# An encoder step: first C/D weights loaded in the stage before, three score blocks counted by GpSimd, ties of all blocks marked by GpSimd

## The chip, the cores and the metric

The kernel runs on one core of a Trainium2 chip, as one program. Times are device microseconds of a whole execution; less is better. Engines: PE is TensorE (matmuls), DVE is VectorE, ACT is ScalarE, POOL is GpSimd, and SP issues most of the DMAs. "Lines" are lines of the kernel before.

## What is computed

Two layers of a streaming encoder over 2048 prompt frames and 64 sample frames of width 1024. The second layer (C/D) projects its input to queries, keys, values, gates and to a small indexer. For every query frame the indexer scores all admissible keys, and the D attention of that frame sees only the 256 keys with the highest scores:

```python
def dsa_attend(q, qi, wi, qpos, k, v, ki, kpos, topk, t5_d):
    dots = jnp.einsum('bqhe,bke->bqhk', qi, ki)
    score = jnp.einsum('bqh,bqhk->bqk', wi, jax.nn.relu(dots))
    score = jnp.where(admissible, score, NEG_INF)
    _, sel = lax.top_k(score, topk)
    ...
```

Where scores are equal to the 256th, `top_k` takes the ones with the smaller index. The kernel needs no index list, only a mask of the selected keys.

## The kernel before

The stages follow each other, each ended by a meeting of all engines: the A/B layer, its attention and its mix; then `mix_out` of the first layer, `index_stage`, `project_cd`, the attentions C and D, and the last mix. The change touches `index_stage` (lines 2346 to 2570), `top_k` (2573 to 2750) and `project_cd` (2753 to 2915).

**Blocks.** The frames are 17 blocks of 128 rows. Blocks 2 to 16 need a selection. `SEL_BLOCKS` lists them as 3 to 11, then 2, then 12 to 16, and n counts along this list; block b has a score tile of 128 partitions and (b + 1) x 128 columns (`widths[n]`), 384 to 2176, 19,200 columns in all.

**index_stage** computes the indexer's projections (`plan.proj`: T units with the 512 columns of `W_t` as weights, N units with `W_n`) and the scores, in an order written out by a planner. The T units of the first 128 weight columns come last (`plan.tail`). SP loads the weights and then stores each unit's result in order.

**project_cd** does two things at once. TensorE (`multiply`, lines 548 and 551) computes 74 units of the C/D projection: 40 T units (four groups of 5 pieces, twice) and 34 N units, 16 matmul records each, in float32, into 8 PSUM banks. ScalarE copies each unit out (`evacuate`, line 2838) and SP stores it (2807). Meanwhile `top_k` finds the 256th largest score of every row.

**The search** (`search`, `signs`) is a bisection over the 32 bits of the float, all blocks at once, with one threshold a row and block in `thr`. In every step VectorE counts the scores that reach the threshold, block by block (line 2621; the first NOWN = 9 of the list, blocks 3 to 11), while ScalarE does it with the sum of signs for the last N_SIGN = 6 (line 2659; blocks 2 and 12 to 16). After the third count VectorE prepares the next trial in `tx` with an XOR (2625) and keeps the last count (`remember`, 2647). At the end it waits for all counts, decides (`pred`, 2629) and sets the thresholds (2638), for which both engines wait.

**The masks** (`masks`, `take_sides`, `leave`, `send`). A tail on VectorE (2667 to 2700) corrects the sign blocks: a count, a mark and a minimum for each of the six. Then a loop over the 15 blocks. VectorE marks the scores equal to the threshold (`ties`, 2707, into one of two `junk` buffers), numbers them by a running sum (2714), works out the room (2719), and selects (2723) with the signs that ScalarE took (2738). ScalarE scales the mask and writes it out (`leave`, 2744), SP sends it. The marks of block n + 1 are made behind the running sum of block n.

**ScalarE's order** is fixed. The evacuations are dealt out to the steps of the search by LEAD and PACE, and those left over to the mask loop, behind the leave of a block. In the search a step's first evacuation stands in front of its fourth sign and the others in front of its last:

```python
        STEPS, LEAD, PACE, EARLY, TILES = 32, 4, 0.56, 4, 6
        while int(LEAD + u * PACE) < STEPS:
            in_step[int(LEAD + u * PACE)].append(u)
            u += 1
```

Before, units 0 to 49 leave during the search, 50 to 53 right after it, 54 to 73 in the mask loop. GpSimd only sets 15 small constants in this stage (2728).

## Time and profile before

| | us |
|---|---|
| median of 3 runs | 3863.88 (3859.64 to 3863.9) |
| profiled execution | 3855.95, span of its instructions 3854.2 |
| TensorE busy | 3611.3 (94%) |
| VectorE busy | 2036.2 (53%) |
| ScalarE busy | 1622.6 (42%) |
| GpSimd busy | 691.1 (18%) |
| project_cd, from its first small constant to the last leave's end | 2306.8 to 2811.0 |

Busy shares are means over the whole kernel. Each stage has limits of its own, and a stage ends when the last of its engines does. TensorE's matmuls are pipelined, so that busy time there includes overlap. The granted clock is TensorE's, as a share of 2.4 GHz.

### The profile page before, as it was taken

To read this page: it belongs to the slowest core of one execution; us is meant where nothing else is said; L and a number is where in the kernel's file an instruction comes from. 1 tells how busy PE (TensorE), PEld (TensorE's weight loads), DVE (VectorE), ACT (ScalarE), POOL (GpSimd) and SP (SyncE) were. 2 spreads that over 40 slices of the span, in tenths; PEclk is the share of its full clock that TensorE was granted. 3 is DMA by queue.
4 is the path that set the end of the run, shared out by engine and by line. 5 is a ranking of instruction groups with operands and counts; after the bars stand their busy time and mean duration, and the time that the engine had idled before them with its cause. 6 is when DMAs were issued, how large, how long until landed. Compare 5 with 4: busy or idle time off the path is not lost. (4 is left out here: it accounts for less than half of the span.)

```text
span 3854.2 us, 50563 instructions
## 1 busy us (share of the span) xinstructions
PE 3611.3 (94%) x17937; PEld 2607.2 (68%) x17937; DVE 2036.2 (53%) x5023; ACT 1622.6 (42%) x2526; POOL 691.1 (18%) x475
## 2 busy tenths in 40 slices
PE   7999999989999999997998979899969899999798
PEld 6899999977776666664886745444446555556576
DVE  3311111128885444443321479999968777777432
ACT  5101100115454344333331469998457444444432
POOL 4110000012222111110431100000022432212342
PEclk9999999989999999998999999999979899999899
DMA  5522222144443222213442111101242411100443
GB/s 159 173 78 69 68 70 68 59 89 103 98 107 93 55 72 70 58 35 111 158 147 80 59 44 51 54 34 65 86 120 80 102 36 40 26 12 20 147 167 120
DMA packets 198855, 316.61 MB, mean 82 GB/s; under 512 B 24776, under 2 KB 140768, under 8 KB 193528
## 3 DMA queue, kind: packets, MB, share of 16 engines
q1 hardware_dynamic: 178928, 252.51, 22.0%
q0 software_dynamic: 12352, 34.36, 3.5%
q10 hardware_dynamic: 7344, 26.74, 1.9%
q8 instruction: 134, 2.20, 0.2%
q14 instruction: 97, 0.79, 0.1%
HBM read 212.89 MB, written 112.23 MB: 84 GB/s over the span
## 5 line engine op out<-in xcount | busy, mean ns | idle before, releaser
L1064 PE MATMUL attAB_p_o<-attAB_pt,attAB_v 128*65 128x512 f32 (+4 forms) x1120 | 432.1, 483 | 3.3 <-ACT attAB_pt L1113 3.3
L1156 DVE TENSOR_REDUCE attAB_mx<-attAB_p_s 128x1 f32<-128x512 f32 (+2 forms) x360 | 209.5, 609 | 298.1 <-PE attAB_p_s L997 187.4
L2621 DVE TENSOR_SCALAR_CACHE_REDUCE cd_junk<-score,cd_thr 128x512 bf16<-128x512 f32 (+8 forms) x288 | 350.4, 1275 | 1.3 <-DVE cd_thr L2638 0.2
L450 DVE COPY ab_stage<-ab_pA 128x256 f32<-128x256 f32 (+2 forms) x118 | 58.6, 496 | 543.2 <-PE ab_pA L208 542.7
L2659 ACT ACTIVATE cd_side<-score,cd_thr 128x384 bf16<-128x384 f32 (+2 forms) x192 | 322.3, 1679 | 24.0 <-DVE cd_thr L2638 16.5
L1040 PE MATMUL attAB_p_t<-attAB_q_a,attAB_k_a 128*128 128x512 f32 (+4 forms) x560 | 301.1, 542 | 12.8 <-DVE attAB_s_t L1203 11.5
L207 PE MATMUL ab_pA<-ab_W_lo,h_hi 128*128 128x256 f32 x1088 | 307.9, 283 | 0.0
L208 PE MATMUL ab_pA<-ab_W_hi,h_lo 128*128 128x256 f32 x1088 | 307.9, 283 | 0.0
L206 PE MATMUL ab_pA<-ab_W_hi,h_hi 128*128 128x256 f32 x1088 | 307.9, 283 | 0.0
L295 ACT ACTIVATE ab_stage<-ab_pA 128x256 f32<-128x256 f32 (+2 forms) x98 | 41.7, 426 | 591.7 <-PE ab_pA L208 578.6
L1713 PE MATMUL attD_p_o<-attD_pt,attD_v 128*65 128x512 f32 (+1 forms) x548 | 281.3, 594 | 1.8 <-ACT attD_pt L1802 1.8
L548 PE MATMUL cd_pA<-hT_cd,cd_W 128*128 128x448 f32 (+1 forms) x640 | 234.8, 530 | 28.3 <-ACT cd_stage L2838 15.2
L1802 ACT ACTIVATE attD_pt<-attD_s_t 128x512 f32<-128x512 f32 (+1 forms) x306 | 178.3, 602 | 154.4 <-DVE attD_s_t L1919 151.4
L551 PE MATMUL cd_pA<-cd_W,hT_cd 128*128 128x512 f32 x544 | 236.2, 596 | 6.2 <-ACT cd_stage L2838 5.6
L1113 ACT ACTIVATE attAB_pt<-attAB_p_t 128x512 f32<-128x512 f32 (+3 forms) x328 | 171.1, 543 | 163.9 <-PE attAB_p_t L1041 114.4
L206 PE MATMUL ab_pA<-h_hi,ab_W_hi 128*128 128x448 f32 (+1 forms) x640 | 229.9, 359 | 7.9 <-DVE ab_W_lo L220 7.9
L2187 PE MATMUL mix_pY<-mix_W_hi,mix_m_hi 128*128 128x512 f32 x544 | 219.5, 404 | 12.1 <-DVE mix_m_lo L2234 12.1
L207 PE MATMUL ab_pA<-h_lo,ab_W_hi 128*128 128x448 f32 (+1 forms) x640 | 228.4, 357 | 0.0
L208 PE MATMUL ab_pA<-h_hi,ab_W_lo 128*128 128x448 f32 (+1 forms) x640 | 228.3, 357 | 0.0
L548 PEld LDWEIGHTS cd_pA<-hT_cd,cd_W 128*128 128x128 f32 x640 | 124.1, 195 | 138.4 <-issue 98.5
L2188 PE MATMUL mix_pY<-mix_W_lo,mix_m_hi 128*128 128x512 f32 x544 | 216.2, 397 | 0.0
L2189 PE MATMUL mix_pY<-mix_W_hi,mix_m_lo 128*128 128x512 f32 x544 | 216.1, 397 | 0.0
(354 smaller groups left out, 8452.0 us busy)
## 6 DMA issues: line engine op xcount, KB each, us to landing
mix_o<-t_o SPq DMA_DIRECT2D x34, 512.0 KB, 4.4
mix_gate<-t_gate SPq DMA_DIRECT2D x68, 256.0 KB, 4.8
ab_W_raw<-in_w_ab SPq DMA_DIRECT2D x16, 1024.0 KB, 5.7
attAB_raw<-t_k SPq DMA_DIRECT2D x30, 544.0 KB, 6.1
attAB_raw<-t_q SPq DMA_DIRECT2D x30, 544.0 KB, 7.9
ab_front<-in_x ACTq DMA_DIRECT2D x17, 512.0 KB, 3.7
t_gate<-ab_stage SPq DMA_DIRECT2D x68, 128.0 KB, 1.7
t_v<-ab_stage SPq DMA_DIRECT2D x68, 128.0 KB, 1.7
```

What stands on the lines that cost most here:

```text
L206: nc.tensor.matmul(out, lh, rh, start=(k == 0), stop=False)
L207: nc.tensor.matmul(out, lh, rl, start=False, stop=False)
L208: last = nc.tensor.matmul(out, ll, rh, start=False, stop=(k == KT - 1))
L548: last = nc.tensor.matmul(pA[s][:, 0:end - begin], W[j % 2][:, k, c * P:(c + 1) * P], hT[:, k, begin:end], start=(k == 0), stop=(k == KT - 1))
L551: last = nc.tensor.matmul(pA[s][:, 0:w], hT[:, k, r * P:(r + 1) * P], W[j % 2][:, k, 0:w], start=(k == 0), stop=(k == KT - 1))
L1040: nc.tensor.matmul(out, hi[:, ks], q_a[j][:, cols], start=(x == 0), stop=False)
L1064: done = nc.tensor.matmul(p_o[u % 2][0:VW, i0 * w:(i0 + n) * w], left, pt[c % NPT][:, at * w:(at + n) * w], start=(c == plan.chunks_of[u][ ...
L1713: nc.tensor.matmul(p_o[u % 2][0:VW, 0:w], left, pt[c % NPT][:, 0:w], start=(c == first), stop=(c == last)).then_inc(valued, 1)
L2187: nc.tensor.matmul(out, m_hi[s][:, k, :], W_hi[:, k, cols], start=(k == 0), stop=False)
L2188: nc.tensor.matmul(out, m_hi[s][:, k, :], W_lo[:, k, cols], start=False, stop=False)
L2621: nc.vector.tensor_scalar(junk[nth % 2][:, 0:widths[n]], sc[n][:], T[:, n:n + 1], None, ALU.is_ge, ALU.add, accum_out=cnt[s % 2][:, n:n + ...
L2659: nc.scalar.activation(side[0][:, 0:widths[n]], sc[n][:], ACT.Sign, bias=T[:, n:n + 1], accum_out=cnt[s % 2][:, n:n + 1]).then_inc(signed, 1)
```

## The change

- `W_t`, the weight tile of the index stage, is now allocated outside and also serves as the first weight buffer of `project_cd`. SP loads the first C/D weights into it during the index stage: three quarters once the last unit that needs the old ones is staged, the last quarter after the last unit. `project_cd` then only signals that they are there.
- N_SIGN is 5, so block 2 is counted by VectorE. The list of blocks stays the same.
- GpSimd counts the first three blocks (3, 4, 5: 512, 640 and 768 columns). It writes 0/1 marks in bfloat16 into the buffer `rank`, padded to 768 columns with zeros, and adds the halves onto each other three times (384, 192, 96 columns for each of the three). VectorE sums the 3 x 96 that are left into the counts. VectorE itself counts blocks 6 to 11 and 2.
- The XOR for `tx` becomes a two-input instruction, an XOR with an OR against a zero tile, and stands after VectorE's third own count.
- In the mask loop GpSimd makes the marks of the ties for all 15 blocks.
- LEAD is 1: units 0 to 55 leave during the search, 56 to 59 right after it, 60 to 73 in the mask loop. A step's first evacuation stands in front of its third sign.

```diff
-N_SIGN = 6
+N_SIGN = 5
-SEL_BLOCKS = [*range(FIRST_SEL + 1, NB - N_SIGN + 1), FIRST_SEL, *range(NB - N_SIGN + 1, NB)]
+SEL_BLOCKS = [*range(FIRST_SEL + 1, NB - N_SIGN), FIRST_SEL, *range(NB - N_SIGN, NB)]
+N_POOL = 3
...
+                after = d.w_cd[0].rearrange("(k p) c -> p k c", p=P)
                 for p, (kind, c, x) in enumerate(plan.proj):
                     sp.wait_ge(staged, p + 1)
+                    if p == plan.tail - 1:
+                        for t in (1, 2, 3):
+                            sp.dma_start(W_t[:, :, t * P:(t + 1) * P], after[:, :, t * P:(t + 1) * P]
+                                         ).then_inc(next_in, 16)
+                    if p == NP - 1:
+                        sp.dma_start(W_t[:, :, 0:P], after[:, :, 0:P]).then_inc(next_in, 16)
...
+    NDVE = NOWN - N_POOL
+    WIDE = (SEL_BLOCKS[N_POOL - 1] + 1) * P
+    HALVINGS = 3
+    LEFT = WIDE >> HALVINGS
+    marks = rank[:].bitcast(BF16)[:, 0:N_POOL * WIDE].rearrange("p (n w) -> p n w", n=N_POOL)
...
-            for n in range(NOWN):
+            for n in range(N_POOL, NOWN):
...
-                if n == 2 and s >= 1:
+                if n == N_POOL + 2 and s >= 1:
                     undo = 3 * 2 ** (bit - 1) if bit >= 1 else 1
-                    nc.vector.tensor_scalar(tx[:], thr[:], undo, None, ALU.bitwise_xor).then_inc(tried, 1)
+                    nc.vector.scalar_tensor_tensor(tx[:], thr[:], undo, none[:], ALU.bitwise_xor, ALU.bitwise_or
+                                                   ).then_inc(tried, 1)
                     remember(dve, s - 1)
-            dve.wait_ge(counted, (s + 1) * NOWN)
+            dve.wait_ge(marked, (s + 1) * (N_POOL + HALVINGS))
+            nc.vector.tensor_reduce(cnt[s % 2][:, 0:N_POOL], marks[:, :, 0:LEFT], AX.X, ALU.add).then_inc(pooled, 1)
+            dve.wait_ge(counted, (s + 1) * NDVE)
+            dve.wait_ge(pooled, s + 1)
             dve.wait_ge(signed, (s + 1) * N_SIGN)
...
+    def count_by_pool(pool):
+        for n in range(N_POOL - 1):
+            nc.gpsimd.memset(marks[:, n, widths[n]:WIDE], 0.0).then_inc(blanked, 1)
+        pool.wait_ge(ready, SETUP)
+        for s in range(STEPS):
+            done = s * (N_POOL + HALVINGS)
+            if s >= 1:
+                pool.wait_ge(turned, s)
+            for n in range(N_POOL):
+                nc.gpsimd.tensor_scalar(marks[:, n, 0:widths[n]], sc[n][:], T[:, n:n + 1], None, ALU.is_ge
+                                        ).then_inc(marked, 1)
+            if s == 0:
+                pool.wait_ge(blanked, N_POOL - 1)
+            for k in range(HALVINGS):
+                half = WIDE >> (k + 1)
+                pool.wait_ge(marked, done + N_POOL + k)
+                nc.gpsimd.tensor_tensor(marks[:, :, 0:half], marks[:, :, 0:half], marks[:, :, half:2 * half], ALU.add
+                                        ).then_inc(marked, 1)
...
-        def ties(n):
-
-            if n >= 2:
-                dve.wait_ge(outed, n - 1)
-            nc.vector.tensor_scalar(junk[n % 2][:, 0:widths[n]], sc[n][:], T[:, n:n + 1], UNIT, ALU.is_equal, ALU.mult
-                                    ).then_inc(equal, 1)
-        ties(0)
...
-            if n + 1 < NSEL:
-                ties(n + 1)
...
+    def ties_by_pool(pool):
+        pool.wait_ge(fixed, 2 + 2 * N_SIGN + 6)
+        pool.wait_ge(counted, STEPS * NDVE + N_SIGN)
+        for n in range(NSEL):
+            if n >= 2:
+                pool.wait_ge(outed, n - 1)
+            nc.gpsimd.tensor_scalar(junk[n % 2][:, 0:widths[n]], sc[n][:], T[:, n:n + 1], UNIT, ALU.is_equal, ALU.mult
+                                    ).then_inc(equal, 1)
...
-        W = [sb(f"W{j}", [P, KT, BANK]) for j in range(2)]
+        W = [W_t, sb("W1", [P, KT, BANK])]
...
-        STEPS, LEAD, PACE, EARLY, TILES = 32, 4, 0.56, 4, 6
+        STEPS, LEAD, PACE, EARLY, TILES = 32, 1, 0.56, 4, 6
...
-                load(0)
+                sp.wait_ge(w_free[0], 1)
+                sp.sem_inc(w_in[0], 16)
                 load(1)
...
-                    at = {3: in_step[s][0:1], N_SIGN - 1: in_step[s][1:]}
+                    at = {2: in_step[s][0:1], N_SIGN - 1: in_step[s][1:]}
...
                 set_widths(pool)
+                count_by_pool(pool)
+                ties_by_pool(pool)
```

## Rows read from the trace of the kernel before

**Rows 1.** Timeline of ScalarE, end of the stage (start us, us, engine, line)

```profile
2808.96 2.01 ACT L2744 ACTIVATE score<-cd_junk 128x2176 bf16<-128x2176 bf16 x1
```

**Rows 2.** The page's groups (count, busy us, mean ns, idle before and releaser)

```profile
L1156 DVE TENSOR_REDUCE attAB_mx<-attAB_p_s 128x1 f32<-128x512 f32 (+2 forms) x360 | 209.5, 609 | 298.1 <-PE attAB_p_s L997 187.4
...
L548 PE MATMUL cd_pA<-hT_cd,cd_W 128*128 128x448 f32 (+1 forms) x640 | 234.8, 530 | 28.3 <-ACT cd_stage L2838 15.2
...
L551 PE MATMUL cd_pA<-cd_W,hT_cd 128*128 128x512 f32 x544 | 236.2, 596 | 6.2 <-ACT cd_stage L2838 5.6
```

**Rows 3.** Timeline of TensorE in the stage, two of its nine pieces

```profile
2315.78 97.38 PE L548 MATMUL cd_pA<-hT_cd,cd_W 128*128 128x320 f32 x272 [12.79 <-DMA cd_W<-in_w_cd]
...
2724.07 84.36 PE L551 MATMUL cd_pA<-cd_W,hT_cd 128*128 128x512 f32 x192 [2.73 <-ACT cd_stage L2838]
```

**Rows 4.** Timeline of VectorE, the tail and the end of the mask loop

```profile
2685.67 0.61 DVE L2672 TENSOR_SCALAR_CACHE_REDUCE cd_junk<-score,cd_thr 128x384 bf16<-128x384 f32 x1
...
2716.37 0.49 DVE L2707 TENSOR_SCALAR cd_junk<-score,cd_thr 128x512 bf16<-128x512 f32 x1
...
2805.00 2.48 DVE L2723 SCALAR_TENSOR_TENSOR cd_junk<-cd_rank,cd_room,cd_side 128x2176 bf16<-128x2176 f32 x1 [0.47 <-DVE cd_room L2719]
```

**Rows 5.** Instructions of line 2638 (min/median/max ns, first and last start)

```profile
L2638 DVE SCALAR_TENSOR_TENSOR cd_thr<-cd_pred,cd_tx x31: 174/174/175, 2330.5 to 2685.1; 128x15 int32<-128x15 int32 x31
```

**Rows 6.** Timeline of VectorE, second step of the search

```profile
2321.61 0.17 DVE L2625 TENSOR_SCALAR cd_tx<-cd_thr 128x15 int32<-128x15 int32 x1
...
2321.76 1.14 DVE L2621 TENSOR_SCALAR_CACHE_REDUCE cd_junk<-score,cd_thr 128x896 bf16<-128x896 f32 x1
...
2330.48 0.17 DVE L2638 SCALAR_TENSOR_TENSOR cd_thr<-cd_pred,cd_tx 128x15 int32<-128x15 int32 x1
```

**Rows 7.** Timeline of ScalarE, the same step

```profile
2319.20 0.61 ACT L2659 ACTIVATE cd_side<-score,cd_thr 128x384 bf16<-128x384 f32 x1 [0.73 <-DVE cd_thr L2634]
...
2319.94 1.68 ACT L2659 ACTIVATE cd_side<-score,cd_thr 128x1664 bf16<-128x1664 f32 x1
...
2329.82 0.18 ACT L2659 ACTIVATION_READ_ACCUMULATOR cd_side<-score,cd_thr 128x1 f32 x1
```

**Rows 8.** Timeline of SP's queue, last stores of the index stage

```profile
2217.29 58.13 SPq L2408 DMA_DIRECT2D t_kq<-ix_stage  x5
```

**Rows 9.** Window of 2 us behind TensorE's gap at 2724 (busy, granted clock)

```profile
2725.00:2727.00 2.00, 2.00 (x4) 0.61 0.29 111
```

**Rows 10.** Groups of GpSimd by form over the whole kernel

```profile
L2145 POOL TENSOR_TENSOR mix_gate<-mix_gate,mix_sig 128x1024 f32<-128x1024 f32 x32 | 76.4, 2389 | 170.7 <-ACT mix_sig L2096 170.7
...
L1573 POOL TENSOR_TENSOR attD_near_t<-attD_bias_t,attD_msk_t 128x1024 f32<-128x1024 f32 x33 | 69.9, 2137 | 182.6 <-ACT attD_msk_t L1778 182.2 <-DVE attD_bias_t L1858 0.4
...
L379 POOL CAST ab_front<-ab_front 8x2176 fp32r<-8x2176 f32 x2 | 4.0, 1993 | 46.9 <-DMA t_logf<-ab_front 43.5 <-DMA t_nf<-ab_front 3.4
```

**Rows 11.** Timeline of VectorE at three places outside the stage

```profile
14.92 1.36 DVE L479 TENSOR_TENSOR ab_wf_lo<-ab_stage,ab_wf_hi 128x64 fp32r<-128x64 f32 x1
...
3017.82 0.69 DVE L1881 CUSTOM_DVE_ANT_0 attD_junk<-attD_p_s,attD_msk 128x512 bf16<-128x512 f32 x1 [0.15 <-PE attD_p_s L1664]
...
3083.85 2.40 DVE L1846 TENSOR_TENSOR attD_c_b<-attD_raw,attD_c_a 64x2048 fp32r<-64x2048 f32 x1
```

**Rows 12.** Timeline of GpSimd at the same places, and one dependent pair

```profile
13.86 2.34 POOL L340 TENSOR_TENSOR h_lo<-ab_front,h_hi 128x1024 fp32r<-128x1024 f32 x1 [0.48 <-ACT h_hi L290]
...
2851.21 2.37 POOL L1554 TENSOR_TENSOR attC_q_a<-attC_q_raw,attC_q_a 64x1024 fp32r<-64x1024 f32 x1 [0.17 <-POOL attC_q_a L1554]
...
3017.65 4.07 POOL L1562 TENSOR_TENSOR attD_near<-attD_bias,attD_msk 128x2048 f32<-128x2048 f32 x1 [3.19 <-DMA attD_bias<-t_bias_d]
...
3084.18 6.02 POOL L1562 TENSOR_TENSOR attD_near<-attD_bias,attD_msk 128x2048 f32<-128x2048 f32 x1
```

**Rows 13.** Groups of VectorE in the mask loop, 2716 to 2815 us

```profile
L2707 DVE TENSOR_SCALAR cd_junk<-score,cd_thr 128x512 bf16<-128x512 f32 (+14 forms) x15 | 13.0, 866 | 4.7 <-ACT score L2744 4.7
...
L2719 DVE TENSOR_SCALAR cd_room<-cd_sums,cd_left 128x1 f32<-128x1 f32 x15 | 3.1, 208 | 3.4 <-ACT cd_side L2738 3.4
```

More of the change, by code:

```diff
@@ L2343, in score, with index_stage @@
         return u + 1
-def index_stage(nc, d, hT, sc):
+def index_stage(nc, d, hT, sc, W_t):
     plan = IndexPlan()
@@ L2354, in index_stage @@
         sb, ps, sem = allocate(nc, st, "ix")
-        W_t, W_n = sb("W_t", [P, KT, BANK]), sb("W_n", [P, KT, VW_W])
+        W_n = sb("W_n", [P, KT, VW_W])
         stage = [sb(f"stage{s}", [P, BANK]) for s in range(2)]
@@ L2367, in index_stage @@
         wn_in, products, staged, adm_in = sem("wn_in"), sem("products"), sem("staged"), sem("adm_in")
+        next_in = sem("next_in")
         stored = [sem(f"stored{k}") for k in range(2)]
@@ L2411, in _ @@
                 wait_stored(sp, NP)
+                sp.wait_ge(next_in, CT * 16)
             @block.gpsimd
@@ L2585, in top_k @@
     zero = sb("zero", [P, 1])
+    none = sb("none", [P, NSEL], I32)
     junk = [sb(f"junk{k}", [P, ROWS], BF16) for k in range(2)]
@@ L2596, in top_k @@
         "fixed", "equal", "ranked", "roomed", "sided", "chosen", "outed", "sent", "widths_set"))
+    marked, blanked, pooled = sem("marked"), sem("blanked"), sem("pooled")
     UNIT = 2.0 ** -12
@@ L2599, in top_k @@
     NOWN = NSEL - N_SIGN
-    SETUP = 5 + N_SIGN
+    NDVE = NOWN - N_POOL
[3 more added lines that the diff above has]
+    marks = rank[:].bitcast(BF16)[:, 0:N_POOL * WIDE].rearrange("p (n w) -> p n w", n=N_POOL)
+    SETUP = 6 + N_SIGN
     T = thr[:].bitcast(F32)
@@ L2606, in search @@
         nc.vector.memset(zero[:], 0.0).then_inc(ready, 1)
+        nc.vector.memset(none[:], 0).then_inc(ready, 1)
         nc.vector.memset(first[:, 0:NOWN], 2 ** 30).then_inc(ready, 1)
@@ L2616, in search @@
                 dve.wait_ge(turned, s)
-            for n in range(NOWN):
-                nth = s * NOWN + n
+            for n in range(N_POOL, NOWN):
+                nth = s * NDVE + n - N_POOL
                 if nth >= 2:
@@ L2663, in masks @@
         tail = slice(NOWN, NSEL)
-        done = STEPS * NOWN
+        done = STEPS * NDVE
         dve.wait_ge(turned, STEPS)
@@ L2748, in send, with project_cd @@
         sp.dma_start(d.select[SEL_BLOCKS[n], :, 0:widths[n]], out[n]).then_inc(sent, 16)
-    return search, signs, masks, set_widths, take_sides, leave, send, sent
-def project_cd(nc, d, hT, sc):
+    return search, count_by_pool, ties_by_pool, signs, masks, set_widths, take_sides, leave, send, sent
+def project_cd(nc, d, hT, sc, W_t):
     with ExitStack() as st:
         sb, ps, sem = allocate(nc, st, "cd")
-        W = [sb(f"W{j}", [P, KT, BANK]) for j in range(2)]
+        W = [W_t, sb("W1", [P, KT, BANK])]
         stage = [sb(f"stage{s}", [P, BANK]) for s in range(2)]
@@ L2763, in project_cd @@
         w_view = lambda j: d.w_cd[j].rearrange("(k p) c -> p k c", p=P)
-        search, signs, masks, set_widths, take_sides, leave, send, sent = top_k(nc, d, sc, sem, sb)
+        search, count_by_pool, ties_by_pool, signs, masks, set_widths, take_sides, leave, send, sent = top_k(nc, d, sc, sem, sb)
         groups = [("T", BANK), ("T", BANK), ("N", BANK), ("N", BANK)]
@@ L2906, in encoder_step @@
         sc = [st.enter_context(nc.sbuf_tensor(f"score{b}", [P, (b + 1) * P], F32)) for b in SEL_BLOCKS]
-        index_stage(nc, d, hT, sc)
-        project_cd(nc, d, hT, sc)
+        W_t = st.enter_context(nc.sbuf_tensor("W_t", [P, KT, BANK], F32))
+        index_stage(nc, d, hT, sc, W_t)
+        project_cd(nc, d, hT, sc, W_t)
     def keys_c(g):
```

## The prediction, made before the changed kernel ran

> **What bounds the kernel now.** Read first the end of the C/D projection stage, since the change touches no other stage's work and only that end can move. Then the page's groups, then the timelines engine by engine. The stage runs from 2306.8 us to the last leaving activation's end at 2810.97 [rows 1], and three engines share it.
>
> TensorE has 471.0 us of projection work in it (234.8 + 236.2) and 34.5 us idle ahead of its parts (28.3 + 6.2) [rows 2], of which the wait for the first weights is 12.8; it ends at 2724.07 + 84.36 = 2808.4 [rows 3]. VectorE ends at 2805.00 + 2.48 = 2807.5 [rows 4]. Two chains end within 1 us of each other: shortening one alone gives little.
>
> VectorE's chain has three parts. The search, 32 steps from 2307.3 to 2685.3: 378.0 us, its threshold updates 354.6 / 30 = 11.82 us apart [rows 5]. In a step without evacuations VectorE is last: from 2319.20 to the next step at 2330.48 + 0.21, 11.49 us, of which 0.45 are the decision (two short instructions) and 11.04 all before it [rows 6]. ScalarE's six signs end at 2330.00 [rows 7]; with 0.5 for the decision its own step would be 11.3. The evacuations (1/0.56, so 1.79 a step from the fifth step on) put ScalarE last: without the two steps that have none the mean is 11.84, so (11.84 - 11.33) / 1.79 = 0.3 us each (an estimate). The tail for the sign blocks: 2685.3 to 2716.4. The mask loop: 2716.37 to 2807.48, 91.1 us [rows 4].
>
> **TensorE's side of the change.** The early load takes the 12.8 us wait away: the matmuls can begin at some 2307.4, where they began at 2315.8 [rows 3]. The four loads stand on SP's queue ahead of stores of the index stage. Its last five stores lie 58.1 / 4, about 14 us apart, the last one issued before 2275.5 and the weights used at 2307 [rows 8], so they cost nothing; without that cover ScalarE's next evacuation would once wait the few us of a 1.5 MB load. LEAD = 1 lets unit u leave at about step 1 + 0.56u, some 6.4 us apart. TensorE needs 234.8 / 40 = 5.9 for a T unit and 236.2 / 34 = 6.9 for an N unit, and eight banks lie between, so the other 21.7 us of idle time (34.5 - 12.8) go too. With each gap goes a restart at a lower granted clock (0.61 over 2 us behind a gap of 2.7, so mostly at 1.2 GHz [rows 3, 9]), some 1.8 us for each of five. TensorE's end: 2307.4 + 471.0 - 9 = 2769.4, 39 us earlier. It stops being the bound, but for the order of ScalarE's queue (below).
>
> **The search.** VectorE loses the three smallest counts, 2.41 us (2319.20 to 2321.61 [rows 6]), and gains block 2, 0.54 (a 0.61 us count, less the overlap that its followers show) [rows 4]: 11.04 - 2.41 + 0.54 = 9.17. A reduce over 3 x 96 elements comes on top. The nearest rows are 0.61 us for up to 512 elements [rows 2], so 0.2 to 0.6; I take 0.4, by its length. With the decision and its hand-over, 0.53, that is 10.1. ScalarE loses the 384-wide sign, 0.74 (2319.20 to 2319.94 [rows 7]): 10.6 + 0.3 x 1.79 = 11.1.
>
> GpSimd, idle in this stage, gets three compares (1920 elements) and three halvings (1152, 576 and 288). The trace has no compare on it. A one-input cast takes 0.92 ns an element (1993 for 2176), two-input operations 2.09 and 2.33 [rows 10]. So a compare costs 0.92 to 2.33. I take 0.95 and 0.15 us fixed, because it is one-input. Compares: done at 2.4 us of the step; halvings 2.5 + 1.3 + 0.7: done at 7.3, ahead of both engines (by the upper bound at 10, level with them).
>
> The short instructions in mid step are not free, though. A VectorE operation with both inputs in SBUF and GpSimd's own exclude each other, whichever is first: a 64-wide subtraction took 1.36 us and ended 0.08 behind GpSimd's, and a GpSimd product took 6.02 in place of 4.07 because it began under a subtraction of VectorE. With one input in PSUM neither is longer (0.69 beside 4.07) [rows 11, 12]. The Trainium skill ("SBUF — State Buffer", section Who interferes with whom) calls this an exclusive lock held for the whole instruction; by that rule, the trace agrees. The section also has it that a count that writes out its accumulator and a reduce don't take the lock, which no row here shows.
>
> The XOR of the thresholds now has two SBUF inputs and comes 3.6 us into the step (three counts from 896 on), inside the first halving (2.5 to 5.0). It waits 1.5 us. The copy behind it gets in before the second halving: GpSimd's dependent operations stand 0.17 apart [rows 12], XOR and copy take 0.15 together [rows 6]. VectorE's step: 9.17 + 1.5 + 0.4 + 0.53 = 11.6, the new bound. Search: 31 x 11.6 + 10.9 for the first = 370.5, so -7.5 us. Both ends: no wait leaves ScalarE's 11.1 (-22); the copy caught by the second halving too gives 13.0 (+36).
>
> **The tail** has one block less: 0.54 for its count and about 1.0 for its mark and minimum over the same 384 elements: -1.6.
>
> **The mask loop.** Removed: the ties on VectorE, 13.0 us; and with ScalarE no longer held up by TensorE the waits of 4.7 and 3.4 [rows 13]. Added: 15 marks on GpSimd, 19,200 elements: 18.2 + 15 x 0.15 = 20.5 us (upper bound 47). They lie in another buffer than the one being scanned, but scan and select both read two SBUF tensors. The buffer of mark n + 1 comes free once block n - 1 has left, at most 2.0 us [rows 1] into scan n; the scan holds GpSimd off, GpSimd runs when it ends and holds the select off. So the marks stay on the chain. They hide only the room step, 0.21 [rows 13] and 0.1 of hand-over in 14 blocks: -4.2. Two more hand-overs a block, 0.08 each [rows 11, 12]: +2.3. Loop: 91.1 - 13.0 - 8.1 - 4.2 + 20.5 + 2.3 = 88.6, so -2.5.
>
> **Sum:** -7.5 - 1.6 - 2.5 = -11.6. The profiled execution took 3855.95, 8 us less than the runs' median of 3863.88; I set the difference against the median: 3852.3. ScalarE reaches the last two evacuations (units 72 and 73, behind the leave of block 13) near 2760 and waits there for TensorE until 2770; the sign it needs next is due just then, so this costs nothing. But it is the floor: with a faster loop that sign, three selects, two marks and two scans still follow 2770, and the gain stops at about 18.
>
> **The rivals.**
> *The scan lets GpSimd in* (its second input is one broadcast element). The marks vanish under the scans, the loop is near 70, the gain at the floor: 3846. Against it: it reads two SBUF tensors as in rows 11. 0.17.
> *Compares run at about 1.7 ns.* They end at 3.9 us, the XOR waits 0.3, ScalarE bounds the step (-22), but the loop's marks are 35 (+12): 3852 to 3857, mostly a gain near the limit of what can be told. 0.12. The Trainium skill ("GPSIMD Engine Reference", section Performance pitfalls for Q7 kernels) has bodies with a compare at 2.03 cycles an element unless unrolled, which would be this case; no row shows it.
> *The short instructions are held longer* (the other side). Compares of 1.3 to 1.5 ns put the XOR at the start of the first halving (wait 2.2 or more), or the copy is caught as well (+1.3). Each us of wait costs 31 in all; from a wait of 1.9 the gain is gone: 3866 to 3895. For it: the 1.36 us of rows 11. 0.26.
> *The counts exclude GpSimd too:* 9 + 7 a step, some +140. 0.02.
> *The parts don't add up:* a wait that I don't see leaves 3858 to 3868. 0.05.
>
> **Numbers.** The forecast has 0.38 and a range of its own, 3848 to 3858. What a measurement can tell from no change is 0.2%, 7.7 us. Faster: 0.32 of the forecast, 0.17, 0.08 of the 1.7 ns case, 0.57. Same: the rest of the forecast and of that case, and the last rival, 0.16. Slower: 0.27. The range 3842 to 3880 takes in the floor and, on the other side, an XOR that waits for the whole first halving.
>
> **What would show it.** TensorE's first projection matmul near 2307 and no gap over 1 us; thresholds 11.6 us apart (11.1: nothing is held; 13: both are); an XOR that lasts about 1.6 us; a 512-wide compare of 0.6 us; selects that last longer, or start later, by the length of a mark; the last leave's end near 2799. Compares above 1.2 ns an element, or scans that let GpSimd in, would make it wrong.

## The result, and the profile after

The changed kernel takes 3868.60 us (median of 20 runs, 3862.89 to 3875.9) where the kernel before takes 3860.57 (20 runs, 3857.27 to 3868.06): a ratio of 1.0019, interval 1.0012 to 1.0026. That is at the edge of what was called "no change", and on the slow side of it: 8 us more, where 11.6 less had been forecast.

Nothing moved ahead of the stage: its first small constants come at 2306.9 us (2306.8 before). At its end, ScalarE's last leave (timeline; before [rows 1]):

```profile
2816.58 2.02 ACT L2787 ACTIVATE score<-cd_junk 128x2176 bf16<-128x2176 bf16 x1 [5.58 <-DVE cd_junk L2756]
```

So it ends at 2818.60, 7.6 us later than before. TensorE (timeline, the first and the last of its four pieces; before [rows 3]):

```profile
2307.52 116.24 PE L549 MATMUL cd_pA<-hT_cd,W_t 128*128 128x320 f32 x320 [4.42 <-ACTq L2874]
...
2655.32 116.97 PE L552 MATMUL cd_pA<-cd_W,hT_cd 128*128 128x512 f32 x272 [0.31 <-PE cd_pA L552]
```

It begins 8.3 us sooner, has no gap over 0.31 us left and ends at 2655.32 + 116.97 = 2772.3, 36 us sooner. It is out of the way. The search (instructions of two lines: min/median/max ns, first and last start; before [rows 5, 6]):

```profile
L2643 DVE SCALAR_TENSOR_TENSOR cd_tx<-cd_thr,cd_none x31: 548/785/789, 2323.1 to 2662.2; 128x15 int32<-128x15 int32 x31
...
L2660 DVE SCALAR_TENSOR_TENSOR cd_thr<-cd_pred,cd_tx x31: 174/175/176, 2330.6 to 2669.7; 128x15 int32<-128x15 int32 x31
```

339.1 / 30 = 11.30 us a step where it was 11.82. The search ends with the last of these updates at 2669.9 (2685.3 before), 15.4 us sooner. GpSimd's timeline of the second step, and VectorE's:

```profile
2330.88 5.60 POOL L2681 TENSOR_SCALAR cd_rank<-score,cd_thr 128x512 bf16<-128x512 f32 x3 [1.06 <-DVE cd_thr L2660]
2336.57 4.54 POOL L2688 TENSOR_TENSOR cd_rank<-cd_rank 128x1152 bf16<-128x1152 bf16 x3
```

```profile
2334.42 0.79 DVE L2643 SCALAR_TENSOR_TENSOR cd_tx<-cd_thr,cd_none 128x15 int32<-128x15 int32 x1
...
2340.02 0.60 DVE L2639 TENSOR_SCALAR_CACHE_REDUCE cd_junk<-score,cd_thr 128x384 bf16<-128x384 f32 x1
...
2341.14 0.45 DVE L2647 TENSOR_REDUCE cd_cnt<-cd_rank 128x3 f32<-128x288 bf16 x1 [0.52 <-POOL cd_rank L2688]
```

The three compares take 5.60 us, not the 2.3 that the forecast gave them, and GpSimd, not VectorE, ends each step: the reduce waits 0.5 us for the last halving. The XOR takes 0.79 where L2660, of the same kind and size, takes 0.17, so it is held 0.6 us rather than 1.5.

The tail goes from 2669.9 to 2699.3, 29.4 us for 31.1 before: 1.7 less. What was gained is lost in the mask loop, 2699.3 to 2816.5. Counted here and below from the tail's last instruction to the end of the last select, it takes 117.3 us for 91.1 before (groups of that stretch: busy, mean ns, idle ahead of it; before [rows 13]):

```profile
L2766 POOL TENSOR_SCALAR cd_junk<-score,cd_thr 128x512 bf16<-128x512 f32 (+14 forms) x15 | 93.6, 6243 | 44.7 <-DVE cd_left L2742 30.5 <-ACT score L2787 13.7
...
L2756 DVE SCALAR_TENSOR_TENSOR cd_junk<-cd_rank,cd_room,cd_side 128x512 bf16<-128x512 f32 (+14 forms) x15 | 56.2, 3748 | 1.6
L2749 DVE TENSOR_TENSOR_SCAN cd_rank<-cd_junk,cd_zero 128x512 f32<-128x512 bf16 (+14 forms) x15 | 42.4, 2826 | 15.5 <-POOL cd_junk L2766 14.9
```

The marks are 93.6 us of work, the scans wait 14.9 us for them, and the selects (L2756) are 56.2 us; how long they are by themselves the first experiment shows. Timelines of GpSimd and of VectorE in the loop:

```profile
2743.62 7.05 POOL L2766 TENSOR_SCALAR cd_junk<-score,cd_thr 128x1536 bf16<-128x1536 f32 x1 [1.75 <-ACT score L2787]
...
2796.73 10.54 POOL L2766 TENSOR_SCALAR cd_junk<-score,cd_thr 128x2176 bf16<-128x2176 f32 x1 [1.35 <-ACT score L2787]
```

```profile
2742.33 3.09 DVE L2749 TENSOR_TENSOR_SCAN cd_rank<-cd_junk,cd_zero 128x1408 f32<-128x1408 bf16 x1
...
2745.63 5.21 DVE L2756 SCALAR_TENSOR_TENSOR cd_junk<-cd_rank,cd_room,cd_side 128x1408 bf16<-128x1408 f32 x1
...
2764.00 3.62 DVE L2749 TENSOR_TENSOR_SCAN cd_rank<-cd_junk,cd_zero 128x1664 f32<-128x1664 bf16 x1 [5.78 <-POOL cd_junk L2766]
```

The mark over 1536 columns starts 1.3 us into a scan, and when the scan has ended, the select behind it takes 5.21 us and ends 0.2 us behind the mark. In sum: -15.4 - 1.7 + 26.1 = +9.0 at the last select, 7.6 at the last leave, which no longer stands behind a product of TensorE's. The spans of the two profiled executions differ by more, 13.9 us; these two lie 1.3 us above and 4.6 us below the medians of their kernels, and the medians differ by 8.0.

### The profile page after: what moved, and what is told of

It reads as the page before. It is cut to its first block and busy times, and to the rows that moved or that the text cites. A ratio compares the mean times of both kernels' runs of the same rounds, so it can differ in the third digit from the quotient of the medians.

```text
span 3868.1 us, 50601 instructions
## 1 busy us (share of the span) xinstructions
PE 3606.4 (93%) x17937; PEld 2606.7 (67%) x17937; DVE 2030.2 (52%) x4907; ACT 1600.1 (41%) x2462; POOL 1105.6 (29%) x684
## 5 line engine op out<-in xcount | busy, mean ns | idle before, releaser
L2701 ACT ACTIVATE cd_side<-score,cd_thr 128x1664 bf16<-128x1664 f32 (+4 forms) x160 | 302.6, 1891 | 28.9 <-DVE cd_thr L2660 21.6
L2639 DVE TENSOR_SCALAR_CACHE_REDUCE cd_junk<-score,cd_thr 128x896 bf16<-128x896 f32 (+6 forms) x224 | 290.5, 1348 | 1.4 <-DVE cd_thr L2660 0.3
L819 POOL DMA_DIRECT2D attAB_v<-t_v x16 | 18.9, 1182 | 889.5 <-ACT attAB_q_a L840 609.3
L207 PEld LDWEIGHTS ab_pA<-ab_W_hi,h_hi 128*128 128x128 f32 x1088 | 208.9, 192 | 0.0
L208 PEld LDWEIGHTS ab_pA<-ab_W_lo,h_hi 128*128 128x128 f32 x1088 | 208.9, 192 | 0.0
```

The source lines that it names most:

```text
L207: nc.tensor.matmul(out, lh, rh, start=(k == 0), stop=False)
L208: nc.tensor.matmul(out, lh, rl, start=False, stop=False)
L2639: nc.vector.tensor_scalar(junk[nth % 2][:, 0:widths[n]], sc[n][:], T[:, n:n + 1], None, ALU.is_ge, ALU.add, accum_out=cnt[s % 2][:, n:n + ...
L2701: nc.scalar.activation(side[0][:, 0:widths[n]], sc[n][:], ACT.Sign, bias=T[:, n:n + 1], accum_out=cnt[s % 2][:, n:n + 1]).then_inc(signed, 1)
```

## The experiments

Each run is compared with runs of the kernel before on the same chip.

### 1 to 4: one part at a time, and the price of an instruction

**e1_ties_vector**: the changed kernel with the ties back where they were.

```diff
+        def ties(n):
...
+        ties(0)
...
+            if n + 1 < NSEL:
+                ties(n + 1)
...
-                ties_by_pool(pool)
```

> The changed kernel with the ties of the mask loop marked by VectorE again; search, early load and LEAD stay as changed. Theory A (the mask loop alone took back what the search gained; its marks cost GpSimd 3.5 us per 1000 columns): the loop falls from 117 to under 100 us. TensorE still ends near 2772, and ScalarE, waiting there for the last two evacuations, holds up the loop's last blocks: last leave's end near 2798, some 20 us under the changed kernel and 12 under the kernel before (3848, ratio 0.997). Theory B (the order of ScalarE's queue costs nothing): last leave near 2785, 3836. Theory C (the loss lies in the later stages, which took 6 us more in the profiled execution): no more than 5 us under the changed kernel.

3846.41 us, 0.9968 (0.9956 to 0.9981), as theory A had it: the loop is 96.9 us and the last leave ends at 2799.5. Theory C, a loss in the later stages, is out. By the two ratios the marks cost the changed kernel 0.5%, 20 us, more than all that its other parts give. The selects are back at their own length (groups of the loop, and two waits of VectorE's in it):

```profile
L2765 DVE SCALAR_TENSOR_TENSOR cd_junk<-cd_rank,cd_room,cd_side 128x512 bf16<-128x512 f32 (+14 forms) x15 | 23.3, 1551 | 1.6
...
L2749 DVE TENSOR_SCALAR cd_junk<-score,cd_thr 128x512 bf16<-128x512 f32 (+14 forms) x15 | 13.0, 869 | 14.0 <-ACT score L2796 13.8
L2891 ACT ACTIVATE cd_stage<-cd_pA 128x512 f32<-128x512 f32 x14 | 8.1, 588 | 25.2 <-PE cd_pA L552 25.2
```

```profile
2748.97 1.08 DVE L2749 TENSOR_SCALAR cd_junk<-score,cd_thr 128x1664 bf16<-128x1664 f32 x1 [5.99 <-ACT score L2796]
...
2762.80 1.15 DVE L2749 TENSOR_SCALAR cd_junk<-score,cd_thr 128x1792 bf16<-128x1792 f32 x1 [7.83 <-ACT score L2796]
```

15 selects take 23.3 us here and 56.2 in the changed kernel. The evacuations' row (L2891) has 25.2 us of idle time, where the changed kernel has 0.3 in its loop and the kernel before 20.8: the loop runs ahead of TensorE again, ScalarE waits at its evacuations, and VectorE behind it for 5.99 + 7.83 us.

**e2_marks_cast**: the changed kernel, each mark replaced by a cast over the same columns.

```diff
-            nc.gpsimd.tensor_scalar(junk[n % 2][:, 0:widths[n]], sc[n][:], T[:, n:n + 1], UNIT, ALU.is_equal, ALU.mult
-                                    ).then_inc(equal, 1)
+            nc.gpsimd.tensor_copy(junk[n % 2][:, 0:widths[n]], sc[n][:]).then_inc(equal, 1)
```

> The changed kernel with GpSimd's marks in the mask loop replaced by plain copies of the scores to bfloat16, same columns and buffers (so the ties are left out and the masks are not the right ones). It gives the step of the prediction with the price that it assumed. Theory A (the price of a compare on GpSimd was the fault, the rest of the loop's sum holds): copies at 0.9 ns a column, loop 88 to 92 us, 26 us under the changed kernel. Theory D (the exclusion of VectorE and GpSimd is the fault, whatever the instruction costs): the copies take several us each beside scans and selects, the loop stays above 105 us.

3847.19 us, 0.9973 (0.9962 to 0.9984). The loop is 96.9 us: 20 less than in the changed kernel, but neither the 88 to 92 of theory A nor the 105 of theory D. With an instruction that runs at the price that the forecast had for the marks (1.58 us for 1664 columns), the loop is as long as with the ties on VectorE, and it too waits for TensorE (28.3 us idle ahead of ScalarE's evacuations, 25.2 in e1). How long it is without those waits is left to e11.

**e3_load_lead**: the kernel before with only the early load and LEAD = 1.

```diff
...
-        STEPS, LEAD, PACE, EARLY, TILES = 32, 4, 0.56, 4, 6
+        STEPS, LEAD, PACE, EARLY, TILES = 32, 1, 0.56, 4, 6
...
-                load(0)
+                sp.wait_ge(w_free[0], 1)
+                sp.sem_inc(w_in[0], 16)
```

> The kernel before with the early load of the first C/D weights and LEAD = 1 alone; counts, signs and ties as before. Theory A: TensorE begins at 2307.5 and ends at 2770, 38 us earlier, but the search still takes 378 us (two more with the six evacuations moved into it) and the loop 83 to 85 instead of 91: 4 to 6 us under the kernel before, ratio 0.9985 to 0.999. Rival: TensorE alone was the bound, then 15 us or more. Rival: nothing, since both waits come back in another place, ratio 1.000.

3852.74 us, 0.9984 (0.9975 to 0.9993), about as expected. TensorE ends at 2773.0, the last leave at 2803.9, 7 us sooner: VectorE's chain is the next bound, close behind.

**e4_probe**: the kernel before, with GpSimd instructions run one after another, each three times, while VectorE counts.

```diff
...
+                done(g.tensor_copy(o, x))
+                done(g.tensor_scalar(o, x, lim[:, 0:1], None, ALU.mult))
+                done(g.tensor_scalar(o, x, 0.25, None, ALU.mult))
+                done(g.tensor_scalar(o, x, lim[:, 0:1], None, ALU.is_ge))
+                done(g.tensor_scalar(o, x, 0.25, None, ALU.is_ge))
+                done(g.tensor_scalar(o, x, lim[:, 0:1], UNIT, ALU.is_equal, ALU.mult))
+                done(g.tensor_scalar(o, x, 0.25, UNIT, ALU.add, ALU.mult))
+                done(g.tensor_tensor(o, x, y, ALU.add))
...
```

> The kernel before with ten kinds of GpSimd instruction, 512 and 1024 columns, three times each, on a scratch buffer while VectorE counts (GpSimd is idle there otherwise). Theory A: a compare with one operation takes about 2.5 ns a column and one with two operations 3.5, also when nothing else uses the port; a cast or a product 0.9 to 1.0; an add of two tensors 1.9 to 2.3 in either type. Theory D: compares are as fast as products here, since only scans and selects hold them up. In both the thresholds stay 11.8 us apart: counts with one input in SBUF don't exclude GpSimd. If they do, the step grows.

One run, 3866.42. GpSimd's groups by form (lines 2745 to 2752 are the eight above, in order; 1024 columns):

```profile
L2750 POOL TENSOR_SCALAR cd_rank<-score,cd_lim 128x1024 bf16<-128x1024 f32 x3 | 11.2, 3723 | 0.3
L2746 POOL TENSOR_SCALAR cd_rank<-score,cd_lim 128x1024 bf16<-128x1024 f32 x3 | 8.6, 2851 | 0.3
L2748 POOL TENSOR_SCALAR cd_rank<-score,cd_lim 128x1024 bf16<-128x1024 f32 x3 | 8.6, 2851 | 0.3
...
L2749 POOL TENSOR_SCALAR cd_rank<-score 128x1024 bf16<-128x1024 f32 x3 | 8.3, 2767 | 0.3
L2752 POOL TENSOR_TENSOR cd_rank<-score 128x1024 bf16<-128x1024 f32 x3 | 7.1, 2358 | 0.2
...
L2751 POOL TENSOR_SCALAR cd_rank<-score 128x1024 bf16<-128x1024 f32 x3 | 3.1, 1044 | 0.3
L2745 POOL CAST cd_rank<-score 128x1024 bf16<-128x1024 f32 x3 | 3.1, 1037 | 0.2
```

With the rows for 512 columns (in the same order 2015, 1572, 1568, 1491, 1273, 617 and 609 ns) the difference over 512 columns gives the price of a column: cast 0.84 ns, sum and product with two constants 0.83, sum of two tensors 2.12, **one operation with a constant or a column of limits 2.50, whether it compares or multiplies**, equality and product with a column of limits 3.34. The expectation had a product at 0.9 to 1.0 ns a column, and that was wrong: the price does not hang on the compare but on the form. The Trainium skill ("GPSIMD Engine Reference", section Performance pitfalls for Q7 kernels) puts the extra cost at bodies with a compare; here a product costs the same 2.8 us.

The thresholds did not all stay 11.8 us apart either: three steps took 13.5 to 13.7. In each of them the XOR (L2625, one input, 15 elements) met GpSimd's sum of two tensors (VectorE's timeline, and GpSimd's):

```profile
2371.37 2.33 DVE L2625 TENSOR_SCALAR cd_tx<-cd_thr 128x15 int32<-128x15 int32 x1
```

```profile
2371.31 2.37 POOL L2752 TENSOR_TENSOR cd_rank<-score 128x1024 bf16<-128x1024 f32 x1
```

An instruction that takes 0.17 us by itself was held to the end of GpSimd's.

### 5 to 8: the parts beside each other

**e5_late_evac**: e1 with the evacuations of the mask loop further apart.

```diff
-        STEPS, LEAD, PACE, EARLY, TILES = 32, 1, 0.56, 4, 6
+        STEPS, LEAD, PACE, EARLY, TILES = 32, 1, 0.56, 4, 9.5
```

> The changed kernel with the ties back on VectorE, and in the mask loop an evacuation for every 9.5 tiles of mask rather than every 6. In the first experiment VectorE's mask loop stood still for 5.99 and 7.83 us because ScalarE, whose queue is in order, waited for TensorE's products (end 2773.8) ahead of a side or a leave. Theory A (the spacing of the evacuations was all that this loop lost): with an evacuation placed only when its product is there, the loop takes the sum of VectorE's own instructions, about 84 us from 2700.6, so the last leave starts at about 2786 rather than 2797.5: 12 us off, 3834 us, ratio to the kernel before 0.9935. Rival B (TensorE takes the time back, since its banks come free later and its own end moves out): TensorE ends at 2780 or later and the time stays at 3845, ratio 0.997.

3834.24 us, 0.9936 (0.9922 to 0.9950), as theory A had it (the loop is 83.3 us), and the fastest kernel here that does all of the computation. ScalarE's timeline ends with

```profile
2781.89 2.02 ACT L2796 ACTIVATE score<-cd_junk 128x2176 bf16<-128x2176 bf16 x1 [4.61 <-DVE cd_junk L2765]
```

15.6 us sooner than in e1, of which some 2 are an earlier start of the loop, and no evacuation waits for TensorE.

**e6_search_only**: the kernel before with the search part alone (the diff is against the changed kernel, and the early load goes with it).

```diff
...
-        W = [W_t, sb("W1", [P, KT, BANK])]
+        W = [sb(f"W{j}", [P, KT, BANK]) for j in range(2)]
...
-        STEPS, LEAD, PACE, EARLY, TILES = 32, 1, 0.56, 4, 6
+        STEPS, LEAD, PACE, EARLY, TILES = 32, 4, 0.56, 4, 6
...
-                ties_by_pool(pool)
```

> The kernel before with the search part alone: five blocks counted by signs on ScalarE, three by GpSimd, four by VectorE; the projection's first weights are loaded where they were, the evacuations begin at step 4 as before, and the ties are VectorE's. Theory A (TensorE's products and the evacuations' place in ScalarE's queue set the end in the kernel before): the search ends some 15 us earlier, but TensorE still begins its products 38 us later than in the changed kernel and ends at 2808, so the last leave starts at 2809 as before: 3860 us, ratio 0.999 to 1.001. Rival B (the mask loop behind the search is what sets the end, whatever TensorE does): the time falls by the 15 us that the search is shorter, 3845 us, ratio 0.996.

3844.13 us, 0.9956 (0.9941 to 0.9971): the time of rival B, but not "whatever TensorE does", for TensorE's end moved with the search. Its timeline (two of eight pieces):

```profile
2575.65 103.27 PE L552 MATMUL cd_pA<-cd_W,hT_cd 128*128 128x512 f32 x240 [1.28 <-ACT cd_stage L2881]
2679.23 116.97 PE L552 MATMUL cd_pA<-cd_W,hT_cd 128*128 128x512 f32 x272 [0.30 <-PE cd_pA L552]
```

It ends at 2796.2, not 2808.4, although its weights come as late as before, because its later gaps were waits for ScalarE's evacuations, which go by the steps of the search: 15.2 and 5.6 us in [rows 2], now 8.5 and 1.3. A faster step pulls TensorE along. The last leave, at 2796.73, still stands behind TensorE's last product.

**e7_ties_only**: the kernel before, its ties marked by GpSimd.

```diff
-            if n + 1 < NSEL:
-                ties(n + 1)
...
+    def ties_by_pool(pool):
...
                 set_widths(pool)
+                ties_by_pool(pool)
```

> The kernel before with the ties of the mask loop marked by GpSimd and nothing else. Theory A (a mark of this form takes 3.5 ns a column alone and stretches VectorE's selects, as in the changed kernel): the loop runs 117 us from 2716.2, so that its last leave starts at about 2833 rather than 2809: 24 us more, 3884 us, ratio 1.006. Rival B (the long loop of the changed kernel came from the counts of the search or from the earlier products beside it, not from the marks): the loop takes 95 us or less and the time stays within 5 us, ratio 1.000 to 1.0015.

3885.38 us, 1.0066 (1.0050 to 1.0081), theory A. The last leave starts at 2835.06, and the groups of the loop are those of the changed kernel: 93.6 for the marks, 56.2 for the selects. The loss belongs to this part alone.

**e8_beside**: e5, with compares of the marks' form run by GpSimd beside its loop, for nobody.

```diff
...
+            for half in range(2):
+                w = widths[n] // 2
+                if n or half:
+                    pool.wait_ge(beside, 2 * n + half)
+                nc.gpsimd.tensor_scalar(spare[:, 0:w], hT[:, n % KT, half * w:(half + 1) * w], T[:, n:n + 1], UNIT,
+                                        ALU.is_equal, ALU.mult).then_inc(beside, 1)
...
```

> The kernel of e5 (ties on VectorE, evacuations every 9.5 tiles), and beside its mask loop GpSimd runs compares of the marks' form, over the same columns, cut in two each, from another tensor into a spare one, for which nobody waits. Theory A (a slow instruction of GpSimd holds off VectorE's selects and ties, not only the scan that waits for its result): the loop grows by 20 us or more over e5's, and selects over 1,400 columns and more take twice their time and more. Rival B (what the changed kernel lost was only the wait for the marks, 3.5 ns a column in a chain): the loop stays within 4 us of e5's, and no VectorE instruction is longer than there.

One run, 3852.60, its span 18.4 us above e5's; the loop began 6 us later there, which is no part of the comparison. Groups of the loop:

```profile
L2758 DVE TENSOR_TENSOR_SCAN cd_rank<-cd_junk,cd_zero 128x512 f32<-128x512 bf16 (+14 forms) x15 | 48.0, 3199 | 1.8 <-DVE cd_junk L2767 0.5
L2767 DVE SCALAR_TENSOR_TENSOR cd_junk<-cd_rank,cd_room,cd_side 128x512 bf16<-128x512 f32 (+14 forms) x15 | 24.2, 1613 | 1.6
L2751 DVE TENSOR_SCALAR cd_junk<-score,cd_thr 128x512 bf16<-128x512 f32 (+14 forms) x15 | 19.4, 1294 | 0.5 <-ACT score L2802 0.5
```

Between the theories: the scans grow by 5.6 us (42.4 in e5), the ties by 6.4 (13.0), the selects by 0.9 only (23.3), 13 us in all. Slow compares beside the loop do lengthen VectorE's work, also a tie with one SBUF input, but each by 0.8 us at most and none by a whole compare. Nor is a compare that is under way when a scan begins stopped by it (GpSimd's timeline, and VectorE's):

```profile
2781.53 4.49 POOL L2781 TENSOR_SCALAR cd_spare<-hT_cd,cd_thr 128x1024 bf16<-128x1024 f32 x1 [0.17 <-POOL cd_spare L2781]
```

```profile
2782.56 5.15 DVE L2758 TENSOR_TENSOR_SCAN cd_rank<-cd_junk,cd_zero 128x2048 f32<-128x2048 bf16 x1
```

The compare began under the last 0.9 us of a select and ran beside the scan for 3.5. It took 0.8 us more than the 3.7 of e4, the scan 0.7 more than its 4.43. The long selects of the changed kernel need something more. There a mark waits under the scan and starts its work together with the select; the rows behind e11 show what follows from that.

### 9 to 11: what the loop is made of

**e9_one_op_mark**: the changed kernel, the mark without the product.

```diff
-            nc.gpsimd.tensor_scalar(junk[n % 2][:, 0:widths[n]], sc[n][:], T[:, n:n + 1], UNIT, ALU.is_equal, ALU.mult
+            nc.gpsimd.tensor_scalar(junk[n % 2][:, 0:widths[n]], sc[n][:], T[:, n:n + 1], None, ALU.is_equal
```

> The changed kernel with GpSimd's mark cut to one operation, the test for equality, without the product with the unit, so that the masks are not the reference's. Theory A (a mark stands still while VectorE scans, and the next scan waits for it, so that a block costs the scan and the mark one after the other: 2.13 + 3.48 ns a column and some 0.65 us, over 19,200 columns 117 us as measured): with a mark of 2.5 ns a column, as the compare by a column of limits took in the fourth experiment, the loop takes 19,200 columns x 4.63 ns + 9.8 us = 98.7 us, and up to 3 us more of waits for TensorE's products; the last leave starts at 2798 to 2801 rather than 2816.6: 3851 us, ratio to the kernel before 0.997 to 0.9985. Rival B (the loop's length lies in the wait for the leave and in the handing over, not in the mark's price): the loop stays above 110 us, ratio 1.0005 and more.

3859.04 us, 0.9995 (0.9986 to 1.0005); the last leave starts at 2808.65. The loop is 107.7 us, 9.6 less than 117.3, where theory A had 15.6 to 18.6 less and rival B 7 less at most: the price of the mark counts, but "scan and mark one after the other" is not what the loop does. VectorE's selects, and the last mark with the select beside it, show it:

```profile
L2756 DVE SCALAR_TENSOR_TENSOR cd_junk<-cd_rank,cd_room,cd_side 128x512 bf16<-128x512 f32 (+14 forms) x15 | 45.4, 3026 | 1.6
```

```profile
2791.03 8.19 POOL L2766 TENSOR_SCALAR cd_junk<-score,cd_thr 128x2176 bf16<-128x2176 f32 x1 [2.21 <-ACT score L2787]
```

```profile
2793.84 7.29 DVE L2756 SCALAR_TENSOR_TENSOR cd_junk<-cd_rank,cd_room,cd_side 128x2048 bf16<-128x2048 f32 x1
```

The mark ends at 2799.22 and the select 1.9 us later, as in the changed kernel (1.8). The chain is VectorE's own: the selects are 10.8 us shorter (56.2 there) and the scans' waits for marks 1.8 shorter (13.1 for 14.9), and some 2 us of that go to new waits for ScalarE, which stands behind TensorE's products.

**e10_mark_after_scan**: the changed kernel, from the third mark on none beside a scan.

```diff
             if n >= 2:
                 pool.wait_ge(outed, n - 1)
+                pool.wait_ge(ranked, n)
```

> The changed kernel in which a mark also waits until the scan of the block before it has ended, so that no mark lies beside a scan. Theory A (beside a scan a mark makes no progress at all): the marks shrink from 4.8 to 3.5 ns a column (2176 columns 7.6 us rather than 10.5) and the loop stays at 117 to 120 us: ratio to the changed kernel 1.000 to 1.001, to the kernel before 1.002 to 1.003. Rival B (a mark goes on beside a scan, only slower): what it did there is now to be done afterwards, up to 1.3 ns a column, 10 to 25 us more, ratio to the kernel before 1.0045 and more.

3873.67 us, 1.0042 (1.0025 to 1.0059). Group of the marks, and the last of them in GpSimd's timeline:

```profile
L2767 POOL TENSOR_SCALAR cd_junk<-score,cd_thr 128x512 bf16<-128x512 f32 (+14 forms) x15 | 69.9, 4661 | 72.8 <-DVE cd_rank L2749 40.0 <-DVE cd_left L2742 30.5 <-ACT score L2788 2.2
```

```profile
2804.02 7.63 POOL L2767 TENSOR_SCALAR cd_junk<-score,cd_thr 128x2176 bf16<-128x2176 f32 x1 [4.63 <-DVE cd_rank L2749]
```

The marks are 69.9 us of work rather than 93.6, and the loop is 121.6 us (2699.3 to 2820.9), 4.3 longer. So of the 23.7 us that marks spent beside scans, at most 4.3 were worth anything: a mark that comes when a scan is running stands still until it ends, as theory A has it. The 2176-wide one takes 7.63 us here, 10.54 in the changed kernel, and 3.11 of that lay beside a scan. By the time alone the two theories are not told apart: 1.0042 lies above A's 1.003 and below B's 1.0045; the marks' rows decide.

**e11_cast_late**: e2 with TILES = 9.5, as in e5.

> The changed kernel with GpSimd's marks replaced by plain casts of the scores to bfloat16, so that the masks are not the reference's, and with an evacuation for every 9.5 tiles of mask as in e5. In the second experiment these casts took 0.92 ns a column, the price that the prediction had for the marks, but the loop also waited up to 14 us for TensorE. Theory A (the prediction had the order of the loop right and the price of the mark wrong): without those waits the loop takes the 88.6 us of the prediction, within 3 us: last leave's start at 2790 to 2793 for a loop begun at 2702, 3839 to 3843 us, ratio to the kernel before 0.995. Rival B (the order was wrong too: handing the buffers between three engines costs more than was counted, or scans let the casts in): the loop takes 94 us and more, 3846 and more (ratio 0.997), or 80 us and less, 3832 (0.9925).

3831.16 us, 0.9926 (0.9909 to 0.9942). Timelines of GpSimd and of VectorE:

```profile
2767.53 4.42 POOL L2766 CAST cd_junk<-score 128x2176 bf16<-128x2176 f32 x1 [3.91 <-ACT score L2786]
```

```profile
2765.73 4.42 DVE L2749 TENSOR_TENSOR_SCAN cd_rank<-cd_junk,cd_zero 128x2048 f32<-128x2048 bf16 x1
...
2770.36 3.73 DVE L2756 SCALAR_TENSOR_TENSOR cd_junk<-cd_rank,cd_room,cd_side 128x2048 bf16<-128x2048 f32 x1
```

The order is the forecast's: the cast starts in the scan, ends 1.80 us behind it, and the select takes 3.73 for 2.35. But the loop is 81.6 us (2699.9 to 2781.6), below theory A's bound and above rival B's 80, and the time is the 3832 that rival B had for a short loop: the forecast's 88.6 had 20.5 for marks where casts left to themselves need 0.84 ns a column, some 16, and 2.3 for hand-overs, where scans follow selects 0.1 us apart. Against e5 it is 3 us, no more than can be told.

**How long a select is held.** Before, a select over 896 columns takes 1.15 us, over 1024 columns 1.28, and over 2048 columns 2.35. In e10, where each starts with a mark over 128 columns more, they take

```profile
2716.96 2.01 DVE L2756 SCALAR_TENSOR_TENSOR cd_junk<-cd_rank,cd_room,cd_side 128x896 bf16<-128x896 f32 x1
...
2723.15 4.86 DVE L2756 SCALAR_TENSOR_TENSOR cd_junk<-cd_rank,cd_room,cd_side 128x1024 bf16<-128x1024 f32 x1
...
2804.06 9.38 DVE L2756 SCALAR_TENSOR_TENSOR cd_junk<-cd_rank,cd_room,cd_side 128x2048 bf16<-128x2048 f32 x1
```

So the added time jumps: 0.86, 3.58 and 7.03 us. All twelve selects of e10 from 640 columns on that have a mark beside them fit one sum to 0.02 us: 0.84 ns for each column of the mark, the price of a cast, and 2.6 us more when the mark has over 1024 columns, 5.2 when it has over 2048. In the changed kernel, where a mark has lain under the scan and gets going a little ahead of the select, it is the same sum less 0.36. With the mark of one operation (e9) it is 1.74 us for each 1024 in place of 2.6, and with casts (e11) nothing. That is close to the part of a mark's price that goes beyond a cast's, 2.50 and 1.66 ns a column, times 1024: 2.56 and 1.70 us. That is how it would be if GpSimd worked through pieces of 1024 columns and the select ran only while it computed on the last. The sum is read from these rows; no run here was made to test it.

## Why the prediction was wrong

**TensorE: right.** 2769.4 forecast, 2772.3 measured, and no gap over 1 us. The 2.9 us between lie in the restarts: 9 us were to go with them, and from its start to its end TensorE took 464.8 us, 6.2 less than the forecast's 471.0. "Shortening one alone gives little" was wrong: the load with its LEAD alone gave 6 us (e3), the search alone 17 (e6). It took two chains for independent that ScalarE's evacuations tie together.

**The search: right in sign, 8 us too small.** A step was to be 11.6 us and is 11.30, by two errors that offset each other. Compares cost 2.50 ns a column and not 0.95, so GpSimd's end of step moved from 7.3 to 10.3 us and became the bound; but the XOR was held 0.6 and not 1.5 us. The halvings were right (4.5 forecast, 4.54 measured), and so were ScalarE (11.1 forecast; it ends 0.1 to 0.4 us ahead of need in most steps, and level in the last ones) and the tail (-1.6 forecast, -1.7 measured). Where in the search the rival "short instructions are held longer" put its 31 us for each us of wait, nothing happened: the copy after the XOR took 0.17 us. That was in part luck: the slow compares put the XOR 0.1 us behind the start of the third compare and not beside a halving, and in e4 an XOR beside a sum of two tensors was held for all of its 2.3 us.

**The mask loop: the step that failed**, "15 marks on GpSimd, 19,200 elements: 18.2 + 15 x 0.15 = 20.5 us (upper bound 47)". By themselves the marks take 69.9 us (e10), 3.5 ns a column and more than the upper bound. That bound was 2.33 ns, from the dearest two-input row of [rows 10]; a form that no row shows was taken to be no dearer than the rows that there were. The rival of 1.7 ns went the right way and not half far enough. With 69.9 in place of 20.5 the forecast's sum gives 138.0 us; measured are 121.6 (e10) and 117.3. The difference, 16 to 21 us, is less than the 23.3 us that the selects take by themselves: most of them run beside the slow marks, against "GpSimd runs when it ends and holds the select off".

**Exclusion.** A scan that is running holds GpSimd off to its end, as the forecast said (e10, e11); a compare that is under way is not stopped by a scan (e8). The Trainium skill ("SBUF — State Buffer", section Who interferes with whom) has the lock held for the whole instruction whichever is first; by that rule, a scan that comes first agrees, and the selects and a scan that comes second do not. In e10 (VectorE's timeline, and GpSimd's):

```profile
2792.28 6.54 DVE L2756 SCALAR_TENSOR_TENSOR cd_junk<-cd_rank,cd_room,cd_side 128x1920 bf16<-128x1920 f32 x1
```

```profile
2792.23 7.16 POOL L2767 TENSOR_SCALAR cd_junk<-score,cd_thr 128x2048 bf16<-128x2048 f32 x1 [4.39 <-DVE cd_rank L2749]
```

the select takes 6.54 us and is done 0.57 before the mark that began with it; its own length is 2.22, so it was neither free nor held to the mark's end. Nor does the XOR wait to the end of a 2.2 us compare over 768 columns: it is held 0.6 us, and 768 columns at 0.84 ns are 0.65. With casts (e11) the select over 2048 columns is held for all but 0.2 us of what is left of the cast. The sum behind e11 covers both, with a cast as a mark that has nothing beyond a cast's price; what GpSimd does in that time was not tried and stays open.

**The parts add up.** Counting on GpSimd with the tail: the last leave ends at 2803.9 in e3 and at 2783.9 in e5, 20 us, of which 19.0 are the search and the tail and 1.0 an earlier start of the stage. From the stage's start the changed kernel has 17.2 there; e3's search is itself 1.5 us longer than the one before, with six more evacuations in it. Marks: +26.1 in the loop of the changed kernel, +26.1 at the last leave of e7. Against what the ties on VectorE cost (13.0 us busy, all of it on the chain), even a mark at a cast's price would have gained no more than the 3 us between e5 and e11.

## What to carry to other kernels

Before work goes to GpSimd, time the exact form of the instruction there, operands and number of operations included: between a cast (0.84 ns a column) and the mark (3.5) lies a factor of four, and neither the number of inputs nor the kind of operation told which it would be. An engine that hands buffers around a ring of three is on the chain though it has idle time (51.7 of the 121.6 us of e10's loop): price a part moved there as if it stood in line. And when a stage has gained time, look at the places of the instructions that pace another engine: the same evacuations, further apart, were worth 12 us (e5).

## What the runs showed of the hardware that was not expected

- GpSimd, by the column of 128 partitions: 2.50 ns for one operation with a constant or a column of limits, 3.34 (e4) and 3.5 (e10) for equality and product with a column of limits, but 0.83 for a sum and a product with two constants.
- A mark that comes while a scan runs makes no progress until it ends (23.7 us of marks beside scans were worth at most 4.3, e10), but a compare that began 1.0 us ahead of a scan ran on beside it for 3.5 us (e8).
- A select that starts with a mark costs the mark nothing (3.70 us over 1024 columns beside a select, 3.72 alone in e4) and is itself held 0.84 ns for each column of the mark, and 2.6 us more beyond 1024 and again beyond 2048 (e10).
- An instruction of VectorE's with one input and 15 elements was held 2.0 to 2.2 us beside GpSimd's sum of two tensors, to its end (e4).
- VectorE's ties with one SBUF input grow from 13.0 to 19.4 us beside a busy GpSimd (e8), while the counts with an accumulator do not grow: over 896 columns 1.15 us beside a compare of GpSimd's, 1.14 before [rows 6].
